# Seven block products of a feed-forward layer: which one comes second, and where the residual rows wait meanwhile

## The chip, the cores and the metric

The kernel runs on one core of one Trainium2 chip. The metric is the device time of one execution in microseconds (us). The engines are TensorE (PE, matrix products; its weight loads are PEld), VectorE (DVE), ScalarE (ACT), GpSimd (POOL) and SyncE (SP), which issues most transfers. Sixteen DMA engines move the data of all queues between device memory and the on-chip memory.

## The reference, cut to what matters

The program is two transformer-like blocks, one after the other, on 512 tokens of width 1024: a mixer block with a mixture of 16 experts, then a block with recurrent branches, a feed-forward layer and a gated embedding. All of it is in float32. The change touches the feed-forward layer of the second block and what stands around it:

```python
D_MODEL, SEQ, PLE_DIM = 1024, 512, 256
D_FF = -(-(8 * D_MODEL) // (3 * 256)) * 256            # 2816
...
    mixed = jax.nn.sigmoid(gate_a) * y_a + jax.nn.sigmoid(gate_b) * y_b
    x = x + mixed @ w_out

    h = _rmsnorm(x, g_ffn)
    x = x + (jax.nn.silu(h @ w1) * (h @ w3)) @ w2      # up products, then the down product

    gate = jax.nn.sigmoid(_rmsnorm(x, g_ple) @ w_ple_gate)
    x = x + gate * (p_i @ w_ple)
    return x                                           # then _rmsnorm(x, g_final)
```

## The kernel before, in words

**Order of the work.** The program is written out by hand for each engine; engines meet only at semaphores. In the profile the experts' matmuls run from 285 to 1190 us, the up products (`h @ w1`, `h @ w3`) from 1638 to 1877 us, the down product (`@ w2`) from there to 1993 us, and the gate product, the final norm and the stores to the end.

**Three passes.** A float32 product is made of three products of rounded numbers. For each operand ACT writes a rounded copy ("high part", `weight_rounded`, `down_rounded`), DVE the difference ("rest", `weight_rest`, `down_rest`), and PE adds high x rest, rest x high and high x high. So a piece of weights that lands must pass ACT, then DVE, before PE can use it.

**The down product** (512 x 2816 times 2816 x 1024) is split 2 x 2 x 2: into 256 tokens, 1408 inner, 512 output columns. Instead of eight block products it makes seven, after Strassen and Winograd, named `p1`, `ue`, `p2`, `wb`, `vg`, `zf`, `hh`. Each is 66 matmuls of 128 x 512 (11 inner tiles, 2 token tiles, 3 passes), in three chunks d = 0, 1, 2 of 24, 24 and 18 matmuls. PE counts a finished chunk in `down_chunk`, so p1's are 1 to 3, the second product's are 4 to 6, and so on. Before its first matmul a chunk waits for its rests (`wlo_made` for weights, `alo_made` for activations).

**Weights.** Blocks of `w2` lie in device memory as three pieces each: two of 128 x 2048 numbers (1024 KB, 1.05 MB) and one of 128 x 1536 (768 KB, 0.79 MB). `p1`, `p2` and `wb` use blocks 0, 2 and 3 as they are ("plain"). Their pieces go through a ring of four slots (`slot(c)`, c % 4): SP issues piece c on its hardware queue when piece c - 4 has been used. `ue`, `vg`, `zf` and `hh` use sums of blocks ("grown"). Those are made by the DMA itself: SP loads one block's piece into `grown[d]` or `joined[d]`, and POOL then issues an accumulating transfer on its own, software, queue (`add_weights`, L717 to L719), which adds a second block to what lies there. `ue` is block 0 + block 1; `vg` adds block 3 to that; `zf` is block 1 + block 3, in `joined`; `hh` adds block 2 to `vg`'s. That makes 12 accumulating transfers, in this order on POOL's queue: three for `ue`, three for `vg`, three for `zf`, three for `hh`, each waiting until its piece has landed and the previous use's rest has been made.

**Where things lie.** The residual rows `x_res` (512 x 1024, 2.1 MB) lie at `LOW`. During the up products they are written aside to device memory (`x_aside`, L2263 to L2265), and `grown[0]` and `grown[1]` are loaded onto their place (L2266 to L2271) and block 1 is added, in the middle of the up products. When the last up product is done, SP loads the rows back to another place (`x_late`, L2272 to L2274), that of the up products' inputs. `grown[2]` lies on a place that p1's rounded activations of chunks 0 and 1 use, so its load waits for `down_chunk` 2 (L2250 to L2253), and its sum for that load.

**ACT and DVE in the down stage.** Both go through the products in order, chunk by chunk: ACT rounds the activations (`round_part`, L2024), then the weights (`round_down`, L2031); DVE makes the two rests (L1626, L1633). From the third product on, ACT's rounded activations overwrite those of a product two before, so it waits until that one is done. DVE also adds finished products to the rows (`down_sums`, L1636 on).

The names that the steps touch: the tuple `DOWN` (L66) sets the order of the products on every engine; SP's loop over pieces is L2244 to L2289.

## Time and profile before

| | us |
|---|---|
| median of 3 runs | 2046.92 (2045.06 to 2048.33) |
| the profiled execution | 2047.97 |
| its span in the profile | 2046.2 |
| PE busy (matmuls) | 1940.0 (95%) |
| DVE / ACT / POOL busy | 787.7 / 543.2 / 126.2 |

The page gives for each engine the busy time in the span and, in 40 slices, how it is spread, with PE's granted clock and the share of the 16 DMA engines that is busy. The profiled execution took 1.77 us more than its span, and 1.05 us more than the median of the three runs. PE is the engine with most to do, but a busy share over the whole span hides single waits; the views used below are the busy time by windows, the timeline of single instructions, the queues' shares, and the issues of transfers.

### The profile page before, as it was taken

To read this page: it belongs to the slowest core of one execution; us is meant where nothing else is said; L and a number is where in the kernel's file an instruction comes from. 1 tells how busy PE (TensorE), PEld (TensorE's weight loads), DVE (VectorE), ACT (ScalarE), POOL (GpSimd) and SP (SyncE) were. 2 spreads that over 40 slices of the span, in tenths; PEclk is the share of its full clock that TensorE was granted. 3 is DMA by queue.
4 is the path that set the end of the run, shared out by engine and by line. 5 is a ranking of instruction groups with operands and counts; after the bars stand their busy time and mean duration, and the time that the engine had idled before them with its cause. 6 is when DMAs were issued, how large, how long until landed. Compare 5 with 4: busy or idle time off the path is not lost.

```text
span 2046.2 us, 22768 instructions
## 1 busy us (share of the span) xinstructions
PE 1940.0 (95%) x9356; PEld 1202.1 (59%) x9356; DVE 787.7 (38%) x1147; ACT 543.2 (27%) x840; POOL 126.2 (6%) x139
## 2 busy tenths in 40 slices
PE   8999999999899897998989799999999999999998
PEld 6868843333233332333333268878888888888786
DVE  6747331101101010100101057595587544446584
ACT  5246320101010000101000046323444332223465
POOL 3432000000000000000000000042000000000100
PEclk9998999999999999999999899999999999999999
DMA  9420789999999999999999943212124223533971
GB/s 274 144 73 17 295 325 429 432 430 426 433 431 429 431 430 429 432 431 428 432 431 429 425 158 144 69 56 65 61 83 144 83 100 127 164 123 113 268 196 66
DMA packets 45513, 534.90 MB, mean 261 GB/s; under 512 B 5488, under 2 KB 5616, under 8 KB 15104
## 3 DMA queue, kind: packets, MB, share of 16 engines
q1 hardware_dynamic: 41216, 514.42, 61.3%
q0 software_dynamic: 4224, 19.46, 4.5%
q8 instruction: 52, 0.85, 0.2%
q14 instruction: 21, 0.17, 0.0%
HBM read 524.39 MB, written 8.39 MB: 260 GB/s over the span
## 4 chain that ended last, share of the span: by engine, by line
PE 64%; DMA 23%; issue 7%; DVE 4%; ACT 1%; SPq 0%; POOL 0%; ACTq 0%; DVEq 0%; POOLq 0%
DMA arena<-in_w_gu_dram 21%; PE bank L2793 14%; PE bank L2818 5%; PE bank L745 3%; PE bank L747 3%; PE bank L746 3%; PE bank L2755 2%; PE bank L1106 2%; PE bank L1107 2%; PE bank L1108 2%; PE bank L2419 2%; PE bank L2421 2%; PE bank L2425 2%; DMA arena<-in_wpack_dram 2%; PE bank L1151 1%
## 5 line engine op out<-in xcount | busy, mean ns | idle before, releaser
L2793 PE MATMUL bank<-arena 128*64 128x512 f32 x2048 | 477.4, 621 | 71.3 <-DMA arena<-in_w_gu_dram 68.4
L2793 PEld LDWEIGHTS bank<-arena 128*64 128x64 f32 x2048 | 161.8, 143 | 362.1 <-issue 349.8
L3290 DVE TENSOR_TENSOR arena<-arena,bank 128x256 f32<-128x256 f32 x64 | 27.0, 421 | 640.3 <-ACT arena L3531 640.3
L2818 PE MATMUL bank<-arena 128*64 128x512 f32 x1024 | 232.5, 595 | 0.6 <-ACT arena L3535 0.6
L3531 ACT ACTIVATE arena<-bank 128x256 f32<-128x256 f32 x64 | 24.6, 384 | 537.7 <-PE bank L2793 537.7
L2818 PEld LDWEIGHTS bank<-arena 128*64 128x64 f32 x1024 | 73.4, 137 | 139.4 <-issue 139.4
L1106 PE MATMUL bank<-input_rounded,weight_rest 128*128 128x512 f32 x352 | 137.1, 390 | 0.0
L1108 PE MATMUL bank<-input_rounded,weight_rounded 128*128 128x512 f32 x352 | 137.0, 389 | 0.0
L1107 PE MATMUL bank<-input_rest,weight_rounded 128*128 128x512 f32 x352 | 136.9, 389 | 0.0
L745 PE MATMUL bank<-input_rounded,weight_rest 128*128 128x512 f32 x312 | 125.8, 403 | 0.0
L747 PE MATMUL bank<-input_rounded,unit_rounded 128*128 128x512 f32 x312 | 122.0, 391 | 0.0
L746 PE MATMUL bank<-mix_rest,unit_rounded 128*128 128x512 f32 x312 | 121.9, 391 | 0.0
L3535 ACT ACTIVATE arena<-bank 128x256 f32<-128x256 f32 x64 | 24.6, 384 | 214.9 <-PE bank L2804 214.9
L1108 PEld LDWEIGHTS bank<-input_rounded,weight_rounded 128*128 128x128 f32 x352 | 66.1, 188 | 13.9
L1106 PEld LDWEIGHTS bank<-input_rounded,weight_rest 128*128 128x128 f32 x352 | 66.1, 188 | 13.6
L1107 PEld LDWEIGHTS bank<-input_rest,weight_rounded 128*128 128x128 f32 x352 | 66.1, 188 | 13.6
L1776 ACT ACTIVATE unit_rounded<-arena 128x1024 fp32r<-128x1024 f32 x45 | 47.3, 1059 | 77.7 <-PE bank L747 62.1
L1570 DVE TENSOR_TENSOR weight_rest<-arena,weight_rounded 128x2048 fp32r<-128x2048 f32 x22 | 50.3, 2292 | 45.7 <-ACT weight_rounded L1996 45.7
L745 PEld LDWEIGHTS bank<-input_rounded,weight_rest 128*128 128x128 f32 x312 | 58.9, 189 | 13.1 <-issue 1.3
L747 PEld LDWEIGHTS bank<-input_rounded,unit_rounded 128*128 128x128 f32 x312 | 58.7, 188 | 12.9
L1200 DVE TENSOR_TENSOR weight_rest<-arena,unit_rounded 128x1024 fp32r<-128x1024 f32 x43 | 53.3, 1244 | 33.2 <-ACT unit_rounded L1776 33.1
L746 PEld LDWEIGHTS bank<-mix_rest,unit_rounded 128*128 128x128 f32 x312 | 59.0, 189 | 11.2
(584 smaller groups left out, 2940.7 us busy)
## 6 DMA issues: line engine op xcount, KB each, us to landing
arena<-in_w_gu_dram SPq DMA_DIRECT2D x47, 4096.0 KB, 28.9
arena<-in_w_d_dram SPq DMA_DIRECT2D x62, 2048.0 KB, 26.6
arena<-in_wpack_dram SPq DMA_DIRECT2D x81, 1024.0 KB, 5.3
arena<-in_w_gu_dram SPq DMA_DIRECT2D x32, 2048.0 KB, 17.8
arena<-in_wpack_dram POOLq DMA_DIRECT2D x8, 1024.0 KB, 12.2
arena<-in_w_d_dram SPq DMA_DIRECT2D x4, 1024.0 KB, 10.2
arena<-in_wpack_dram SPq DMA_DIRECT2D x5, 768.0 KB, 10.7
arena<-in_w_gu_dram SPq DMA_DIRECT2D x3, 1024.0 KB, 8.6
```

The source lines that it names most:

```text
L745: mm(b, wl[:, k, :], hhi[k], start=k == 0, stop=False)
L746: mm(b, wh[:, k, :], chlo[k], start=False, stop=False)
L747: last = mm(b, wh[:, k, :], hhi[k], start=False, stop=k == KD - 1)
L1106: mm(b, wl[:, k, m], hhi[k], start=k == 0, stop=False)
L1107: mm(b, wh[:, k, m], hlo[k], start=False, stop=False)
L1108: last = mm(b, wh[:, k, m], hhi[k], start=False, stop=k == KD - 1)
L1200: tt(out=unit_lo(j), in0=unit_raw(j), in1=unit_hi(j), op=ALU.subtract).then_inc(S("ulo_made"), 1)
L1570: tt(out=wlo[(c + which) % R], in0=w, in1=whi[(c + which) % R], op=ALU.subtract)\
L1776: fn(unit_hi(j), unit_raw(j), ACT.Copy).then_inc(S("uhi_made"), 1)
L2419: mm(b, wh[:, k, m], hhi[k], start=k == 0, stop=False)
L2793: last = mm(ab[64 * x:64 * x + 64, :], xsT[:, k, 64 * x:64 * x + 64], w[x][k], start=k == 0, stop=k == KD - 1)
L2818: last = mm(bank[4 + n][64 * x:64 * x + 64, :], hidT[c % 2][:, P * t + 64 * x:P * t + 64 * x + 64], w[:, x, t, 512 * n:512 * n + 512], sta ...
```

## The change

`p2`, a product with plain weights, comes second, and `ue`, with grown weights, third. The residual rows are no longer written aside: `x_res` stays at `LOW` for the whole layer and every later use reads it there (`x_late` is gone, and with it one transfer of 2.1 MB each way). `grown[0]` and `grown[1]` therefore lie where the up products' inputs were, and are loaded only after the last up product, directly after p1's third piece; POOL's first three accumulating transfers follow their landings. The rounded activations of `p2`, `ue`, `wb` and `vg` change places with one another. `joined[0]`'s load also waits for the first sum in `grown[0]`, and `joined[2]`'s moves from before `wb`'s second piece to behind `joined[1]`'s. Counts of `down_added` follow the order of the sums. The diff, without the further renamings of `x_late` to `x_res`:

```diff
--- before.py
+++ after.py
@@ -63,7 +63,7 @@
 BLK = HT * TOK
 
 
-DOWN = ("p1", "ue", "p2", "wb", "vg", "zf", "hh")
+DOWN = ("p1", "p2", "ue", "wb", "vg", "zf", "hh")
 DOWN_GROWN = ("ue", "vg", "zf", "hh")
 DOWN_WEIGHT = {"p1": 0, "p2": 2, "wb": 3}
 DOWN_KS = (range(0, 4), range(4, 8), range(8, HT))
@@ -184,7 +184,7 @@
     "pool_landing2": (("fnet_in", 80), ("added_in2", 64)),
     "landing1": (("xT_in1", 16), ("half_in1", 16), ("last_in1", 16), ("grown_in1", 32)),
     "landing3": (("first_in0", 16), ("place_in", 16), ("x_back", 16)),
-    "landing4": (("first_in1", 16), ("x_parked", 16), ("x_late_in", 16), ("ple_back", 16)),
+    "landing4": (("first_in1", 16), ("ple_back", 16)),
     "landing5": (("first_in2", 16), ("gfin_in", 16)),
     "landing6": (("xT_in3", 16), ("wple_in", 16), ("grown_in2", 32)),
     "landing2": (("xT_in2", 16), ("extra_in", 48)),
@@ -210,7 +210,6 @@
         bank += [two_banks[:, 0:512], two_banks[:, 512:1024]]
         named = {}
         ple_kept = nc.dram_tensor("ple_kept", (P, NT * D), F32, kind="Internal").ap()
-        x_aside = nc.dram_tensor("x_aside", (NT, P, D), F32, kind="Internal").ap()
         x_kept = nc.dram_tensor("x_kept", (NT, P, D), F32, kind="Internal").ap()
 
         def S(name):
@@ -524,7 +523,7 @@
         part_of = {"p1": "a11", "ue": "u", "p2": "a12", "wb": "w", "vg": "v", "zf": "z", "hh": "a22"}
         part_lo = {m: [rounded(f"down_rest_{m}_{d}", part_at[name] + TOK * ks[0], TOK * len(ks)) for d, ks in enumerate(DOWN_KS)]
                    for m, name in part_of.items()}
-        hi_at = {"ue": T0 + 1280, "p2": part_at["a11"], "wb": part_at["u"], "vg": part_at["a12"], "zf": part_at["w"],
+        hi_at = {"p2": T0 + 1280, "ue": part_at["a11"], "wb": part_at["a12"], "vg": part_at["u"], "zf": part_at["w"],
                  "hh": part_at["v"]}
         part_hi = {m: [rounded(f"down_rounded_{m}_{d}", at + TOK * ks[0], TOK * len(ks)) for d, ks in enumerate(DOWN_KS)]
                    for m, at in hi_at.items()}
@@ -532,9 +531,8 @@
                      (6, 7, rounded("down_rounded_p1_6", B + 19712, TOK)), (7, 8, rounded("down_rounded_p1_7", T0 + 256, TOK)),
                      (8, 11, rounded("down_rounded_p1_8", T0 + 512, 3 * TOK))]
         first_his_upto = (1, 4, 5)
-        grown = [view(LOW, WCH), view(LOW + WCH, WCH), view(LOW + 9088, 3 * 512)]
+        grown = [view(LOW + 4096, WCH), view(LOW + 4096 + WCH, WCH), view(LOW + 9088, 3 * 512)]
         joined = [view(T0 + 512, WCH), view(B, WCH), view(T0 + 2560, 3 * 512)]
-        x_late = view(LOW + 4096, NT, D)
         pieces = [view(B + 19712 + 512 * i, 512) for i in range(2)]
         down_bank = {"p1": (4, 5), "ue": (6, 7), "p2": (2, 3), "wb": (4, 5), "vg": (0, 1), "zf": (2, 3), "hh": (0, 1)}
 
...
@@ -1125,7 +1123,7 @@
             def turn_tokens(half, ks):
                 for k in ks:
                     for i in range(2):
-                        last = turn(turned_place(half, k)[:, P * i:P * i + P], x_late[:, 2 * half + i, P * k:P * k + P], ident)
+                        last = turn(turned_place(half, k)[:, P * i:P * i + P], x_res[:, 2 * half + i, P * k:P * k + P], ident)
                     last.then_inc(S("norm_turned"), 1)
 
             for m, name in enumerate(DOWN):
@@ -1138,7 +1136,7 @@
                             pe.wait_ge(S("p1_copied"), nth("p1_copied", 2))
                             pe.wait_ge(S("down_added"), nth("down_added", 2))
                         elif name == "zf":
-                            pe.wait_ge(S("down_added"), nth("down_added", 8))
+                            pe.wait_ge(S("down_added"), nth("down_added", 4))
                         elif name == "hh":
                             pe.wait_ge(S("down_added"), nth("down_added", 12))
                     pe.wait_ge(S("alo_made"), rests_upto(m, d))
...
@@ -1643,7 +1641,6 @@
                 b = [bank[j][:, :] for j in down_bank[name]]
                 dve.wait_ge(S("down_chunk"), 3 * m + 3)
                 if name == "p1":
-                    dve.wait_ge(S("x_late_in"), nth("x_late_in", 16))
                     for i in range(2):
                         dve.wait_ge(S("p1_copied"), nth("p1_copied", i + 1))
                         add_down(out_part(i, 0), out_part(i, 0), b[i], ALU.add)
@@ -1657,7 +1654,7 @@
                     for i in range(2):
                         add_down(out_part(i, 0), out_part(i, 0), b[i], ALU.add)
                 elif name == "wb":
-                    dve.wait_ge(S("down_added"), nth("down_added", 6))
+                    dve.wait_ge(S("down_added"), nth("down_added", 8))
                     for i in range(2):
                         add_down(out_part(i, 1), out_part(i, 1), b[i], ALU.subtract)
                 elif name == "vg":
...
@@ -2260,24 +2257,18 @@
                         .then_inc(S(f"chunk_in{c % R}"), 16)
                 else:
                     sp.dma_start(slot(c), wpack[from_dram(c)]).then_inc(S(f"chunk_in{c % R}"), 16)
-                if c == C_UP + 9:
-                    sp.wait_ge(S("out2_added"), nth("out2_added", 8))
-                    sp.dma_start(x_aside.rearrange("i p d -> p i d"), x_res).then_inc(S("x_parked"), 16)
-                if c == C_UP + 13:
-                    sp.wait_ge(S("norm_turned"), 2 * KD)
-                    sp.wait_ge(S("norm_sq"), NT * (N4 + 1))
-                    sp.wait_ge(S("x_parked"), nth("x_parked", 16))
+                if c == C_DOWN + 2:
+                    sp.wait_ge(S("up_filled"), 2 * NFT)
                     for d in range(2):
                         sp.dma_start(grown[d], wpack[C_DOWN + d]).then_inc(S(f"grown_in{d}"), 16)
-                if c == C_DOWN + 2:
-                    sp.wait_ge(S("up_filled"), 2 * NFT)
-                    sp.dma_start(x_late, x_aside.rearrange("i p d -> p i d")).then_inc(S("x_late_in"), 16)
                 if c == C_DOWN + 9:
-                    for d in (0, 2):
-                        sp.dma_start(joined[d], wpack[C_DOWN + 3 + d][:, 0:512 * len(DOWN_KS[d])]).then_inc(S(f"grown_in{d}"), 16)
+                    sp.wait_ge(S("added_in0"), nth("added_in0", 16))
+                    sp.dma_start(joined[0], wpack[C_DOWN + 3]).then_inc(S("grown_in0"), 16)
                 if c == C_DOWN + 11:
                     sp.wait_ge(S("down_chunk"), 9)
-                    sp.dma_start(joined[1], wpack[C_DOWN + 4]).then_inc(S("grown_in1"), 16)
+                    for d in (1, 2):
+                        sp.wait_ge(S(f"added_in{d}"), nth(f"added_in{d}", 16))
+                        sp.dma_start(joined[d], wpack[C_DOWN + 3 + d][:, 0:512 * len(DOWN_KS[d])]).then_inc(S(f"grown_in{d}"), 16)
                 if c == C_OUT2 + 1:
                     sp.wait_ge(S("oT_filled"), 8)
                     sp.wait_ge(S("x_kept"), 16 * NT)
```

SP's issues from p1's third piece (128x1536, the first row) to the load of `joined[1]` (the last row); in brackets the semaphores waited for. Before:

```order
L2259 DMA arena<-in_wpack_dram 128x1536 [waits up_filled]
L2274 DMA arena<-x_aside 128x4x1024 [waits up_filled]
L2253 DMA arena<-in_wpack_dram 128x1536 [waits down_chunk]
L2259 DMA arena<-in_wpack_dram 128x2048 [waits down_chunk] x2
L2259 DMA arena<-in_wpack_dram 128x1536 [waits down_chunk]
L2259 DMA arena<-in_wpack_dram 128x2048 [waits down_chunk]
L2277 DMA arena<-in_wpack_dram 128x2048
L2277 DMA arena<-in_wpack_dram 128x1536
L2259 DMA arena<-in_wpack_dram 128x2048 [waits down_chunk]
L2259 DMA arena<-in_wpack_dram 128x1536 [waits down_chunk]
L2280 DMA arena<-in_wpack_dram 128x2048 [waits down_chunk]
```

Here L2274 is the load of the residual rows and L2253 that of `grown[2]`. After:

```order
L2256 DMA arena<-in_wpack_dram 128x1536 [waits up_filled]
L2263 DMA arena<-in_wpack_dram 128x2048 [waits up_filled]
L2263 DMA arena<-in_wpack_dram 128x2048
L2256 DMA arena<-in_wpack_dram 128x2048 [waits up_filled]
L2256 DMA arena<-in_wpack_dram 128x2048 [waits down_chunk]
L2256 DMA arena<-in_wpack_dram 128x1536 [waits down_chunk]
L2250 DMA arena<-in_wpack_dram 128x1536 [waits down_chunk]
L2256 DMA arena<-in_wpack_dram 128x2048 [waits down_chunk]
L2266 DMA arena<-in_wpack_dram 128x2048 [waits pool_landing0]
L2256 DMA arena<-in_wpack_dram 128x2048 [waits down_chunk]
L2256 DMA arena<-in_wpack_dram 128x1536 [waits down_chunk]
L2271 DMA arena<-in_wpack_dram 128x2048 [waits pool_landing1,down_chunk]
```

L2263 is now the loads of `grown[0]` and `grown[1]`. They stand ahead of the next row, the first piece of the second product, which waits for no chunk of the down stage; its second and third piece wait for `down_chunk` 1 and 2. `grown[2]` (L2250) stands behind them, and one `joined` load fewer (L2266, L2271) stands ahead of `wb`'s second piece.

On ACT, from p1's third weight piece (`weight_rounded_120`, 117, 118, ... are the four slots of the high parts) to the copy of p1's result. Before:

```order
L2024 ACTIVATE down_rounded_ue_142<-arena 128x1024 [waits up_filled,dve_parts]
L2031 ACTIVATE weight_rounded_118<-arena 128x2048 [waits pool_landing0,up_filled]
L2024 ACTIVATE down_rounded_ue_143<-arena 128x1024 [waits up_filled,dve_parts]
L2031 ACTIVATE weight_rounded_119<-arena 128x2048 [waits pool_landing1,down_chunk]
L2024 ACTIVATE down_rounded_ue_144<-arena 128x768 [waits up_filled,dve_parts]
L2031 ACTIVATE weight_rounded_120<-arena 128x1536 [waits pool_landing2,down_chunk]
L2060 ACTIVATE arena<-bank 128x512 [waits act_made,down_chunk]
L2060 ACTIVATE arena<-bank 128x512
L2024 ACTIVATE down_rounded_p_0_145<-arena 128x1024 [waits down_chunk,dve_parts]
L2031 ACTIVATE weight_rounded_117<-arena 128x2048 [waits chunk_in0]
```

After:

```order
L2021 ACTIVATE down_rounded_p_0_142<-arena 128x1024 [waits up_filled,dve_parts]
L2028 ACTIVATE weight_rounded_118<-arena 128x2048 [waits chunk_in1]
L2021 ACTIVATE down_rounded_p_1_143<-arena 128x1024 [waits up_filled,dve_parts]
L2028 ACTIVATE weight_rounded_119<-arena 128x2048 [waits chunk_in2]
L2021 ACTIVATE down_rounded_p_2_144<-arena 128x768 [waits up_filled,dve_parts]
L2028 ACTIVATE weight_rounded_120<-arena 128x1536 [waits chunk_in3]
L2057 ACTIVATE arena<-bank 128x512 [waits act_made,down_chunk]
L2057 ACTIVATE arena<-bank 128x512
L2021 ACTIVATE down_rounded_ue_145<-arena 128x1024 [waits down_chunk,dve_parts]
L2028 ACTIVATE weight_rounded_117<-arena 128x2048 [waits pool_landing0,down_chunk]
```

The weights of the second product's chunks wait for ring pieces (`chunk_in`) in place of POOL's sums (`pool_landing`); the copies of p1's result and then `ue` stand behind them.

## Rows read from the trace of the kernel before

**Rows 1.** Windows: busy us (xinstructions) by engine, PEclk, DMA share, GB/s.

```profile
1750.00:1876.00 126.00, 126.00 (x558) 104.33 (x557) 63.01 (x79) 30.07 (x26) 1.75 (x2) 1.00 0.37 129
1892.90:1914.40 21.50, 17.48 (x67) 13.96 (x66) 9.22 (x8) 8.68 (x8) 3.45 (x4) 0.84 0.97 247
1908.00:1913.00 5.00, 5.00 (x12) 3.94 (x13) 5.00 (x5) 5.00 (x4) 0.84 (x1) 0.52 1.05 276
```

**Rows 2.** Timeline of PE, down stage: start us, us, instruction, [idle, releaser].

```profile
1892.90 0.39 PE L1151 MATMUL bank<-weight_rounded,down_rest_ue 128*128 128x512 f32 x1
...
1903.55 0.39 PE L1153 MATMUL bank<-weight_rounded,down_rounded_ue 128*128 128x512 f32 x1
...
1907.96 0.76 PE L1151 MATMUL bank<-weight_rounded,down_rest_ue 128*128 128x512 f32 x1 [4.02 <-DVE weight_rest L1633]
...
1913.06 0.40 PE L1151 MATMUL bank<-weight_rounded,down_rest_ue 128*128 128x512 f32 x1
...
1914.44 0.40 PE L1151 MATMUL bank<-weight_rounded,down_rest_p 128*128 128x512 f32 x1
...
1935.21 0.47 PE L1151 MATMUL bank<-weight_rounded,down_rest_wb 128*128 128x512 f32 x1 [0.20 <-DVE weight_rest L1633]
```

**Rows 3.** Timeline of ACT, down stage.

```profile
1882.94 1.49 ACT L2031 ACTIVATE weight_rounded<-arena 128x1536 fp32r<-128x1536 f32 x1 [2.21 <-DMA arena<-in_wpack_dram]
...
1904.54 1.48 ACT L2031 ACTIVATE weight_rounded<-arena 128x1536 fp32r<-128x1536 f32 x1 [13.87 <-DMA arena<-in_wpack_dram]
...
1930.82 1.92 ACT L2031 ACTIVATE weight_rounded<-arena 128x2048 fp32r<-128x2048 f32 x1 [3.96 <-DMA arena<-in_wpack_dram]
```

**Rows 4.** Timeline of DVE, down stage.

```profile
1932.77 2.29 DVE L1633 TENSOR_TENSOR weight_rest<-arena,weight_rounded 128x2048 fp32r<-128x2048 f32 x1 [3.40 <-ACT weight_rounded L2031]
```

**Rows 5.** Timeline of SP, the hardware queue's issues; a row of several spans all.

```profile
1747.21 0.80 SPq L2262 DMA_DIRECT2D arena<-in_wpack_dram  x2
1748.13 1.05 SPq L2271 DMA_DIRECT2D arena<-in_wpack_dram  x2
...
1877.77 0.33 SPq L2259 DMA_DIRECT2D arena<-in_wpack_dram  x1
...
1878.14 0.43 SPq L2274 DMA_DIRECT2D arena<-x_aside  x1
...
1920.09 5.77 SPq L2259 DMA_DIRECT2D arena<-in_wpack_dram  x2
```

**Rows 6.** Timeline of POOL, issues of the accumulating transfers.

```profile
1757.23 0.90 POOL L718 DMA_DIRECT2D arena<-in_wpack_dram  x1 [335.89 <-DMA arena<-in_wpack_dram]
1759.69 0.85 POOL L718 DMA_DIRECT2D arena<-in_wpack_dram  x1 [1.57 <-DMA arena<-in_wpack_dram]
1893.63 2.60 POOL L718 DMA_DIRECT2D arena<-in_wpack_dram  x3 [133.09 <-DMA arena<-in_wpack_dram]
...
1926.96 0.86 POOL L718 DMA_DIRECT2D arena<-in_wpack_dram  x1 [17.77 <-DMA arena<-in_wpack_dram]
```

**Rows 7.** DMA queues from 1751 to 1757 us: packets, MB, share of 16 engines.

```profile
q1 hardware_dynamic: 354, 2.51, 99.2%
```

**Rows 8.** DMA queues from 1761 to 1769 us.

```profile
q0 software_dynamic: 219, 1.66, 102.7%
```

**Rows 9.** DMA queues from 1903 to 1915 us.

```profile
q0 software_dynamic: 230, 1.73, 69.3%
q1 hardware_dynamic: 233, 1.56, 32.5%
```

**Rows 10.** DMA queues from 1921 to 1929 us.

```profile
q1 hardware_dynamic: 482, 3.28, 97.4%
q0 software_dynamic: 23, 0.05, 3.1%
```

**Rows 11.** DMA issues from 1757 to 1758 us: size each, us to landing.

```profile
arena<-in_wpack_dram POOLq DMA_DIRECT2D x1, 1024.0 KB, 7.8
```

**Rows 12.** DMA issues from 1903 to 1904.5 us.

```profile
arena<-in_wpack_dram SPq DMA_DIRECT2D x1, 768.0 KB, 13.3
```

More of the change, by code:

```diff
@@ L1635, in out_part @@
             def out_part(i, n):
-                return x_late[:, i, 512 * n:512 * n + 512]
+                return x_res[:, i, 512 * n:512 * n + 512]
             def add_down(out_, in0, in1, op):
@@ L1730, in second_dve @@
                 own.wait()
-                xs = x_late[:, i, 512 * n:512 * n + 512]
+                xs = x_res[:, i, 512 * n:512 * n + 512]
                 tt(out=xs, in0=xs, in1=g, op=ALU.add).then_inc(S("pg_added"), 1)
@@ L1734, in second_dve @@
                     dve.wait_ge(S("pg_added"), nth("pg_added", 7))
-                    own(tt(out=hn[:, NT - 1, 0:512], in0=x_late[:, NT - 1, 0:512], in1=grow[:, 0:512], op=ALU.mult))
-                    own(tt(out=hn[:, i, :], in0=x_late[:, i, :], in1=grow, op=ALU.mult))
+                    own(tt(out=hn[:, NT - 1, 0:512], in0=x_res[:, NT - 1, 0:512], in1=grow[:, 0:512], op=ALU.mult))
+                    own(tt(out=hn[:, i, :], in0=x_res[:, i, :], in1=grow, op=ALU.mult))
                     norm_var(dve, NO, i)
@@ L1758, in second_dve @@
                     norm_rstd(dve, own, NO, i)
-                    stt(out=hn[:, i, :], in0=x_late[:, i, :], scalar=nstat[NO][:, i:i + 1], in1=grow, op0=ALU.mult,
+                    stt(out=hn[:, i, :], in0=x_res[:, i, :], scalar=nstat[NO][:, i:i + 1], in1=grow, op0=ALU.mult,
                         op1=ALU.mult).then_inc(S("out_made"), 1)
@@ L2040, in down_square @@
                 act.wait_ge(S("norm_sq"), NT * N5 + i)
-                act.activation(junk, x_late[:, i, :], ACT.Square, accum_out=nstat[N5][:, i:i + 1]).then_inc(S("norm_sq"), 1)
+                act.activation(junk, x_res[:, i, :], ACT.Square, accum_out=nstat[N5][:, i:i + 1]).then_inc(S("norm_sq"), 1)
             for f in range(NFT):
@@ L2086, in second_act @@
                     act.wait_ge(S("pg_added"), nth("pg_added", 6))
-                    own(fn(junk[:, 0:512], x_late[:, NT - 1, 0:512], ACT.Square, accum_out=v))
+                    own(fn(junk[:, 0:512], x_res[:, NT - 1, 0:512], ACT.Square, accum_out=v))
                     own.wait()
@@ L2100, in second_act @@
                     act.wait_ge(S("norm_sq"), NT * NO + i)
-                    fn(junk[:, 512:D], x_late[:, i, 512:D], ACT.Square, accum_out=stat[:, 342:343]).then_inc(S("norm_sq"), 1)
+                    fn(junk[:, 512:D], x_res[:, i, 512:D], ACT.Square, accum_out=stat[:, 342:343]).then_inc(S("norm_sq"), 1)
                     act.wait_ge(S("norm_var"), NT * NO + NT)
@@ L2109, in second_act @@
                     v = nstat[NO][:, i:i + 1]
-                    fn(junk, x_late[:, i, :], ACT.Square, accum_out=v).then_inc(S("norm_sq"), 1)
+                    fn(junk, x_res[:, i, :], ACT.Square, accum_out=v).then_inc(S("norm_sq"), 1)
                     if i < NT - 2:
```

## The prediction

> **What bounds the kernel now.** I read the page first: PE is busy 95% of the span, so only PE's waits and its pace count. Then the busy time by windows. In the up products PE is busy 126.0 of 126.0 us, with the 16 DMA engines at 0.37 [rows 1]: the transfer that parks the residual rows and the first sums run there beside PE and cost nothing, so taking them out gives nothing there. In the window of `ue` PE is busy 17.5 of 21.5 us, while the DMA share is 0.97. Then the timeline of PE: 48 matmuls start between 1892.90 and 1903.55, one per 0.227 us, so a product of 66 should take 15.0 us. `ue` takes 1914.44 - 1892.90 = 21.5 us, 6.6 us too much [rows 2]. Of it 4.0 us is a wait for DVE's rest of the third piece, and DVE waited for ACT, ACT 13.9 us for the DMA [rows 3]. After the wait the granted clock is 0.52 over 5 us [rows 1], the lower level of 1.2 GHz: the 12 matmuls from 1907.96 to 1913.06 take 5.1 us for 2.7, another 2.4 us. The only other wait in the stage is 0.2 us at `wb`'s second chunk, whose piece was issued at 1920.09 and landed at 1930.82, 10.7 us later [rows 2, 3, 5]. So PE bounds the stage, and its waits are set by transfers.
>
> **What the change removes.** The wait at `ue`'s third chunk and its clock loss: 6.6 us. `ue` now starts a product later, while its third piece is still loaded at `down_chunk` 2, 15 us more in which to land and be summed. With 15 us against a wait of 4.0 I take this term in full.
>
> The load of the parked rows (2.1 MB) goes from the start of the stage, but `grown[0]` and `grown[1]` (2.1 MB) take its place in the queue, and their two sums come into the stage. That is the price, and I work it out at three places.
>
> **Prices of a transfer.** The hardware queue alone moves 2.51 MB in 6 us at 99% share, 0.418 MB/us, so a piece of 1.05 MB takes 2.5 us [rows 7]. Sums alone move 1.66 MB in 8 us at a full share, 0.208 MB/us [rows 8]: 5.0 us a piece, twice as much of the same engines. Together they got 0.130 (hardware) and 0.144 MB/us (sums) over 12 us [rows 9]: a plain piece then takes 8.1 us, 5.6 us more than alone. From landing to PE a piece of 1.05 MB takes 4.4 us through ACT and DVE (1930.82 to 1935.21), one of 0.79 MB 3.4 us (1904.54 to 1907.96) [rows 2 to 4].
>
> **Place A, p2's first piece.** The order on SP is now p1's third piece, `grown[0]`, `grown[1]`, then this piece. The same pattern of four loads stands in the up products: issued from 1747.21 on, the third landed at 1757.23 and the fourth at 1759.69 (POOL's issues follow the landings) [rows 5, 6]. From 1877.77, with the first load 0.79 MB (0.6 us less), the fourth lands 11.9 us later, at 1889.6. PE can start `p2` at 1894.0 and wants it at 1892.9: wait 1.1 us. This holds if the first sum, issued at about 1884.7 when `grown[0]` lands, does not slow it. In two places a sum came late into a busy hardware queue: issued at 1926.96, the sums moved only 0.05 MB between 1921 and 1929 against 3.28 MB [rows 6, 10]. So I take 1.1 us; bounds 1.1 and 6.7 (5.6 us more).
>
> **Place B, p2's second piece.** Undisturbed it lands 2.5 us later, 1892.1, and is ready before its time (1894.0 + 5.4 = 1899.4): 0. But now two sums of 1.05 MB, 10 us of engine time, are in flight. At the shared rate it is 5.6 us later: 1897.7, PE at 1902.1, a wait of 2.7 us. I take 2.7, the nearest row being the shared one [rows 9]; bounds 0 and 4. The third piece lands 0.79 / 0.130 = 6.1 us after that, 1903.8, ready at 1907.2, wanted at 1907.5: just covered. `ue`'s first weights stand behind it on ACT; between 1903.8 and `ue`'s turn at 1911.6 ACT has 1.5 + 1.9 us and DVE 2.3 us of weights to do [rows 3, 4] and three small steps: I cost it at nothing, at most 1 us.
>
> **Place C, wb's second piece.** It is issued when the product before `wb` has done its first chunk, three chunks (15.0 us) before its use, so it may take 15.0 - 4.4 = 10.6 us to land. Before it took 10.7 (the 0.2 us wait), with the sums silent for 8 of these us [rows 10]. Now POOL cannot issue `vg`'s three sums before `ue`'s rests are made, 15 us later than before, so their 2.9 MB (14 us of engine time alone, 20 us at the shared rate) fall on this load; against this, one load of 0.79 MB fewer stands ahead. The slowest load that shared with sums took 13.3 us [rows 12]: wait 2.7, of which 0.2 was there, so 2.5 us. Bounds: 0, and 6.4, if the three loads (3.15 MB) run at 0.130 MB/us until the sums end after 20 us and then alone, landing 17 us after the issue.
>
> The whole ledger says the same. From 1879 to the landing of `wb`'s third piece the engines had 11.3 MB of loads and 3.7 MB of sums, 27.0 + 17.7 = 44.7 us of work; now it is 10.5 and 5.8 MB, 25.1 + 27.8 = 52.9 us. Without any wait that piece would be wanted at 1892.9 + 15.0 + 15.0 + 10.9 - 3.4 = 1930.4, 51.4 us after 1879. Before, there were 6.7 us to spare, now none. `wb`'s third piece I cost at nothing beyond this, since a wait at the second gives it that time. The later sums (`zf`, `hh`) have the queue to themselves in both kernels; they move with PE, and I take 0.
>
> **Clock.** A wait of 4.0 us cost 2.4 us of lower clock; 0.2 us cost none [rows 2]. For waits of 1.1, 2.7 and 2.7 us nothing shows it; bounds 0 and 4.8, I take one fall, 2.4 us.
>
> **The sum.** 1.1 + 2.7 + 2.5 + 2.4 = 8.7 us added, 6.6 us removed: +2.1 us. On the profiled execution's own 2047.97 that gives 2050.1; it stands 1.05 above the median of the runs, so against 2046.92 I predict 2049.0.
>
> **Rival 1: the loads keep ahead of the sums.** If sums only get what a busy hardware queue leaves, as from 1921 to 1929 [rows 10], B, C and the clock cost nothing: 1.1 - 6.6 = -5.5 us, 2041.4. Against it: from 1903 to 1915 the sums took 69% of the engines [rows 9]. The Trainium skill ("DMA: Bandwidth & Descriptors", on the anatomy of one DMA on the GpSimd path) fits 2.0 us plus bytes over 436 GB/s for such a transfer, 4.4 us for 1.05 MB. By that the sums' work would halve, the ledger would close, and this rival would be likely; the trace has 7.8 us for one accumulating transfer with little beside it [rows 11], and the measurement decides.
>
> **Rival 2, slower: the first sum shares from its start.** It begins 1.5 us after its issue (7.8 us to landing less 5.0 us of data leaves 2.8 for both ends [rows 8, 11]), at 1886.2, just when p2's first piece gets its turn. That piece then lands at 1895.2, PE starts `p2` at 1899.6: A is 6.7. The second piece lands at 1902.4, when the two sums (14.6 us) have ended, ready 1906.8 for 1905.0: B 1.8. With C 2.5 and two clock falls 4.8: 15.8 - 6.6 = +9.2, 2056.1. It decides from where p2's first piece lands after 1890. For it: the equal split in [rows 9]; against it the late start in [rows 10]. The Trainium skill ("DMA: Bandwidth & Descriptors", "Queues, rings and completion order") has each engine take turns between its queues packet by packet; by this rule the result is this rival's. The trace agrees with it from 1903 to 1915 and not from 1921 to 1929.
>
> **Rival 3: the change moves the wait but not away from ue.** POOL sums in order, so `ue`'s third sum stands behind two others; issued at some 1907 and 7.8 us long, it lands at 1915, ready 1918.4 for 1922.5. If it missed by the 4 us that it has, the old wait would be back and the prices with it: about +6, 2053.
>
> **How the numbers follow.** Three runs of this kernel spread over 0.16%, so 0.2% (4.1 us) is about what a measurement can tell. Forecast 0.42, its own range from -2 (B and the clock nothing) to +6 (C at its bound): 0.34 of it lies within 0.2%, 0.08 above. Rival 1 0.25: 0.21 faster, 0.04 the same. Rival 2 0.27 and rival 3 0.06, slower. That makes faster 0.21, same 0.38, slower 0.41. The range reaches to rivals 1 and 2, 2041 to 2056.5.
>
> **What would show it.** Right: no PE wait before `ue`'s third chunk; a short wait before p2's first chunk; waits before p2's second and `wb`'s second chunk of 2 to 3 us with a window of clock 0.5 behind one; the up products unchanged at 126 of 126 us; the DMA share near 1 from 1880 to 1937. Wrong: p2's first piece landing after 1890 (rival 2), or its second by 1895 and `wb`'s second within 10.7 us of its issue (rival 1). If PE waits in `zf` or `hh`, the cover that I counted there is gone.

## The result and the profile after

| | us |
|---|---|
| before, median of 11 runs | 2047.45 (2045.06 to 2049.66) |
| after, median of 11 runs | 2053.67 (2049.1 to 2055.01) |
| ratio after / before | 1.0025, 95% interval 1.0017 to 1.0033 |
| the profiled executions | 2047.97 and 2053.49 |
| their spans | 2046.2 and 2051.7 |

The change makes the kernel slower by 0.25%, 5.1 us on the 2046.92 shown before it (the medians alone differ by 6.2). 2049.0 was predicted: the sign of the sum was right, its size too small.

"Stage" below is the time from SP's issue of p1's third piece to the end of `zf`'s third chunk. It grew from 98.97 us to 103.42 us, by 4.46 us. The other 1.07 us of the 5.5 us between the two profiled executions lie ahead of the stage, which begins at 1878.84 for 1877.77 [rows 5]. In the profiled executions of four kernels below that keep the rows parked, and so do the same work as before up to there, it begins between 1877.42 and 1880.04; so the 1.07 us are within the scatter of single executions and no effect of the change.

Windows of after (columns as in [rows 1]): a stretch of the up products, p2's waits, the end of the wait in `wb`, the matmuls right behind it, and all stretches up to there.

```profile
1750.00:1876.00 126.00, 126.00 (x558) 104.36 (x557) 63.23 (x80) 30.06 (x26) 0.00 (x0) 1.00 0.26 99
1893.90:1913.60 19.70, 15.50 (x68) 12.23 (x66) 12.84 (x10) 11.56 (x11) 0.85 (x1) 1.00 0.88 221
1928.80:1949.00 20.20, 15.51 (x62) 12.44 (x61) 10.15 (x9) 11.15 (x9) 0.85 (x2) 0.92 0.99 280
1939.00:1943.00 4.00, 3.83 (x10) 3.14 (x11) 1.89 (x3) 2.51 (x3) 0.00 (x0) 0.57 1.05 298
1880.00:1937.00 57.00, 50.20 (x217) 40.05 (x215) 32.62 (x28) 25.94 (x22) 6.00 (x7) 1.00 0.95 276
```

The up products run exactly as before, 126.00 of 126.00 us [rows 1]; the share of the DMA engines there fell from 0.37 to 0.26. In the last row, from 1880 to 1937, that share is 0.95.

PE's timeline in after, all rows of the stage up to `vg` with a wait for a DVE rest:

```profile
1896.57 0.47 PE L1149 MATMUL bank<-weight_rounded,down_rest_p 128*128 128x512 f32 x1 [2.44 <-DVE weight_rest L1631]
...
1904.03 0.47 PE L1149 MATMUL bank<-weight_rounded,down_rest_p 128*128 128x512 f32 x1 [1.75 <-DVE weight_rest L1631]
...
1939.17 0.77 PE L1149 MATMUL bank<-weight_rounded,down_rest_wb 128*128 128x512 f32 x1 [4.69 <-DVE weight_rest L1631]
```

These are the places A, B and C of the prediction, and no others: `ue`, `zf` and `hh` wait for nothing. Against [rows 2], where `ue` waited 4.02 us, the wait at `ue` is gone, A and B are new, and the wait at C has grown from 0.20 us. Behind C the matmuls run at the lower level of the clock (0.57 in the window): eight of them take 3.5 us for 1.9, so 1.6 us are lost. Behind A and B the clock stays at its full level here.

ACT in after, at the landings behind A, B (its first two rows) and C (the last row):

```profile
1892.18 1.92 ACT L2028 ACTIVATE weight_rounded<-arena 128x2048 fp32r<-128x2048 f32 x1 [5.79 <-DMA arena<-in_wpack_dram]
...
1899.64 1.92 ACT L2028 ACTIVATE weight_rounded<-arena 128x2048 fp32r<-128x2048 f32 x1 [4.60 <-DMA arena<-in_wpack_dram]
...
1920.04 1.92 ACT L2028 ACTIVATE weight_rounded<-arena 128x2048 fp32r<-128x2048 f32 x1 [3.01 <-DMA arena<-in_wpack_dram]
...
1934.79 1.91 ACT L2028 ACTIVATE weight_rounded<-arena 128x2048 fp32r<-128x2048 f32 x1 [11.88 <-DMA arena<-in_wpack_dram]
```

SP in after; L2263 issues `grown[0]` and `grown[1]`, L2266 `joined[0]`, and the row at 1919.55 is `wb`'s second and third piece:

```profile
1878.84 0.33 SPq L2256 DMA_DIRECT2D arena<-in_wpack_dram  x1
1879.21 0.91 SPq L2263 DMA_DIRECT2D arena<-in_wpack_dram  x2
1880.16 10.25 SPq L2256 DMA_DIRECT2D arena<-in_wpack_dram  x3
...
1913.85 0.33 SPq L2256 DMA_DIRECT2D arena<-in_wpack_dram  x1
1914.22 0.43 SPq L2266 DMA_DIRECT2D arena<-in_wpack_dram  x1
1919.55 5.77 SPq L2256 DMA_DIRECT2D arena<-in_wpack_dram  x2
```

POOL in after; the first two rows are `ue`'s first two sums, the last three `vg`'s:

```profile
1886.73 0.90 POOL L716 DMA_DIRECT2D arena<-in_wpack_dram  x1 [464.32 <-DMA arena<-in_wpack_dram]
1889.22 0.85 POOL L716 DMA_DIRECT2D arena<-in_wpack_dram  x1 [1.59 <-DMA arena<-in_wpack_dram]
...
1914.18 0.84 POOL L716 DMA_DIRECT2D arena<-in_wpack_dram  x1 [5.37 <-DVE weight_rest L1631]
1917.52 0.85 POOL L716 DMA_DIRECT2D arena<-in_wpack_dram  x1 [2.50 <-DVE weight_rest L1631]
1920.06 0.85 POOL L716 DMA_DIRECT2D arena<-in_wpack_dram  x1 [1.68 <-DVE weight_rest L1631]
```

The three sums of `vg`, each released by a rest of `ue`, stand around the issue of `wb`'s second piece at 1919.55; before, POOL was silent for the first 7 us after that issue [rows 6]. The queues of after from 1916 to 1934:

```profile
q0 software_dynamic: 295, 2.15, 58.0%
q1 hardware_dynamic: 432, 3.10, 44.4%
```

Both together fill the engines (102%), with the sums taking more than half of the share for less than half of the bytes. This window begins before the sums move. From 1920 to 1934 alone, the sums have 278 packets and 69% of the engines, the hardware queue 273 packets and 34%. The piece issued at 1919.55 lands at 1934.79, 15.2 us later, for 10.7 before [rows 3, 5]. That is place C.

### The profile page after: what moved, and what is told of

Its sections match the earlier page's. It is cut to its first block, busy times and chain, and to the rows that moved or that the text cites. A ratio compares the mean times of both kernels' runs of the same rounds, so it can differ in the third digit from the quotient of the medians.

```text
span 2051.7 us, 22766 instructions
## 1 busy us (share of the span) xinstructions
PE 1939.9 (95%) x9356; PEld 1203.6 (59%) x9356; DVE 788.9 (38%) x1147; ACT 543.5 (26%) x840; POOL 126.0 (6%) x139
## 4 chain that ended last, share of the span: by engine, by line
PE 71%; DMA 23%; DVE 4%; ACT 1%; issue 1%; SPq 0%; ACTq 0%; DVEq 0%
DMA arena<-in_w_gu_dram 21%; PE bank L2784 14%; PE bank L2809 5%; PE bank L1104 4%; PE bank L1105 4%; PE bank L1106 4%; PE bank L743 3%; PE bank L745 3%; PE bank L744 3%; PE bank L2746 2%; PE bank L2410 2%; PE bank L2412 2%; PE bank L2416 2%; DMA arena<-in_wpack_dram 1%; PE bank L1149 1%; PE bank L1150 1%
## 6 DMA issues: line engine op xcount, KB each, us to landing
arena<-in_w_d_dram SPq DMA_DIRECT2D x62, 2048.0 KB, 26.6
arena<-in_w_gu_dram SPq DMA_DIRECT2D x32, 2048.0 KB, 16.7
```

## The experiments

Each kernel ran on the same chip as the kernel before, in three groups; before had medians of 2048.25, 2048.0 and 2048.17 us there. Kernels of different groups are best compared by their ratios to before (0.1% is 2 us). "Waits" are PE's in the stage. Stage and waits come from one profiled execution of each kernel, which can lie some us from the median: 3.9 us above it for after with the sums held, 3.3 and 3.2 us below it for rows stay alone and for `vg`'s sums small.

| kernel | median us | ratio to before, 95% | stage us | waits us |
|---|---|---|---|---|
| before | 2047.45 | | 98.97 | ue 4.02, wb 0.20 |
| after | 2053.67 | 1.0025 (1.0017 to 1.0033) | 103.42 | p2 2.44, 1.75; wb 4.69 |
| order alone | 2050.38 | 1.0011 (1.0002 to 1.0020) | 100.96 | p2 1.84; wb 4.00 |
| rows stay alone | 2053.67 | 1.0028 (1.0019 to 1.0037) | 103.92 | ue 5.03, 0.64; p2 0.20, 0.56; wb 1.90 |
| after, plain piece first | 2053.31 | 1.0029 (1.0018 to 1.0039) | 103.78 | p2 0.45; ue 0.17; wb 8.36 |
| after, grown loads later | 2052.69 | 1.0024 (1.0015 to 1.0033) | 102.61 | ue 3.21; wb 5.57 |
| after, `joined[0]` later | 2048.63 | 1.0006 (0.9997 to 1.0014) | 99.50 | p2 2.37, 0.18; wb 0.65; vg 1.36 |
| after, ue's sums small | 2048.39 | 1.0001 (0.9992 to 1.0010) | 99.47 | p2 1.67; wb 2.26, 1.22 |
| after, vg's sums small | 2047.36 | 0.9992 (0.9983 to 1.0001) | 96.75 | p2 2.32, 1.76 |
| order alone, vg's sums held | 2045.67 | 0.9992 (0.9983 to 1.0001) | 96.97 | p2 1.80; vg 1.08 |
| after, vg's sums held | 2052.81 | 1.0020 (1.0011 to 1.0028) | 106.54 | p2 2.25, 1.81; wb 6.52 |
| order, held, plain first, joined later | 2044.66 | 0.9982 (0.9973 to 0.9990) | 95.95 | wb 2.13 |
| the same, joined last | 2041.41 | 0.9965 (0.9953 to 0.9978) | 93.06 | vg 0.91 |
| the same, rows stay | 2045.97 | 0.9992 (0.9983 to 1.0000) | 96.81 | p2 0.26, 0.19, 0.22; wb 1.71; vg 1.16 |

**1. The change in two halves.** Order alone: before with the new order, and the rows still parked.

```diff
-DOWN = ("p1", "ue", "p2", "wb", "vg", "zf", "hh")
+DOWN = ("p1", "p2", "ue", "wb", "vg", "zf", "hh")
```

> The kernel before with one part of the change: p2 second and ue third (with the places of the rounded activations and of the joined loads that this asks for). The residual rows are still parked in device memory and grown[0] and grown[1] are still loaded and summed during the up products. Theory T (the order pays for itself; the price of the change is the two grown loads and their two sums, moved into the stage): no wait at p2 (0 instead of 2.4 and 1.8 us in the changed kernel) and none at ue, wb's second chunk waits 0 to 2 us; 5 to 7 us faster than before, about 2041.5. Theory U (the order itself costs, since vg's sums now fall on wb's pieces): wb's second chunk still waits 4 to 5 us and the clock falls, so about the time before, 2046 to 2048.

Rows stay alone: after with the old tuple, so the rows stay, and grown loads and their sums fall into the stage.

> The other half of the change alone: the residual rows stay on chip, grown[0] and grown[1] are loaded and summed from the end of the up products, but ue stays second. Theory T: ue's first sum lands some 17 us after the end of the up products, so PE waits about 6 us before ue's first chunk and about 4 us before its third, with the clock falling behind each; later waits as before: 6 to 10 us slower than before, about 2055. If the parked rows' transfers cost anything, less by that. With the order alone at +2.1 us, a sum of the two halves would be +8 to +12 us; the changed kernel has +5 to +6, so the order should save part of what the late sums cost.

Order alone did not gain: it is 0.11% slower. It frees `ue` of its wait, but `wb`'s first piece, issued at 1911.84, lands at 1926.38, 14.5 us later, beside the three sums that `ue`'s rests have just released. PE, then POOL, of order alone:

```profile
1930.77 0.76 PE L1151 MATMUL bank<-weight_rounded,down_rest_wb 128*128 128x512 f32 x1 [4.00 <-DVE weight_rest L1633]
```

```profile
1907.37 0.84 POOL L718 DMA_DIRECT2D arena<-in_wpack_dram  x1 [7.85 <-DVE weight_rest L1633]
1910.70 0.85 POOL L718 DMA_DIRECT2D arena<-in_wpack_dram  x1 [2.50 <-DVE weight_rest L1633]
1913.24 0.84 POOL L718 DMA_DIRECT2D arena<-in_wpack_dram  x1 [1.68 <-DVE weight_rest L1633]
```

So the wait of 4.0 us was moved to `wb`, clock loss included, by the order and without the grown loads. Neither theory had the 1.84 us at p2's first chunk. There is no sum beside that piece; it stands behind the load of the rows, 2.1 MB, and lands 12.7 us after the start of the stage. In after it stands behind the grown loads, also 2.1 MB, and lands after 13.3 us.

Rows stay alone costs 0.28%; `ue` waits 5.03 us at its first chunk, about as expected, but only 0.64 us at its third for some 4. With both, the cost is no larger than with the second alone: the order takes `ue` out of the way of its late sums, and gives that back in `wb`.

**2. Places A and B.** In the first kernel p2's first piece goes ahead of the grown loads, in the second these go behind all three of p2's pieces.

```diff
-                if c == C_DOWN + 2:
+                if c == C_DOWN + 3:      # grown loads later: C_DOWN + 5
                     sp.wait_ge(S("up_filled"), 2 * NFT)
                     for d in range(2):
                         sp.dma_start(grown[d], wpack[C_DOWN + d])...
```

> The changed kernel with p2's first piece issued ahead of the loads of grown[0] and grown[1]. Theory T (the queue's order and its sharing with the sums decide): the wait before p2's first chunk (2.4 us) is gone, but p2's second piece still stands behind the two grown loads, so its wait grows from 1.8 to about 4.2 us and the time stays within 1 us of the changed kernel (or 1 to 2 us slower if the clock falls). If only the first piece mattered, 2.4 us faster than the changed kernel.

> The changed kernel with the loads of grown[0] and grown[1] behind all three pieces of p2 (they are then issued at down_chunk 2, some 11 us later). Theory T: both waits of p2 are gone (4.2 us); ue's first sum lands some 4 us before it is wanted, so ue does not wait; wb's second chunk waits as in the changed kernel, 4 to 6 us with the clock falling: 3 to 4.5 us faster than the changed kernel, about 2049.7. Rival (the sums are late now): ue waits 2 to 5 us and nothing is gained.

With the plain piece first, 4.19 us of waits at p2 become 0.45, and with the later loads none. So A and B come from what stands ahead of p2's pieces and runs beside them. For A that is mostly the 2.1 MB ahead: with the order alone the wait is 1.84 us, and with `ue`'s sums small (in 3) it is 1.67. B is the sums: with them small it is gone, with the grown loads in place. Neither of the two kernels here helped the time. In the first the wait came back in `wb`, whole; in the second it came back at `ue` (3.21 us) and in `wb` (5.57). PE of plain piece first:

```profile
1938.94 0.77 PE L1149 MATMUL bank<-weight_rounded,down_rest_wb 128*128 128x512 f32 x1 [8.36 <-DVE weight_rest L1631]
```

8.36 is 4.69 plus the 3.7 us gained earlier, and `wb`'s second chunk starts 60.5 us into the stage for 60.3. With PE earlier, the pieces have no less work of the engines ahead of them. This is what the prediction's ledger says (52.9 us of work for 51.4 us of time). The expectation of the first kernel had the time right and the place wrong (p2's second chunk); in the second kernel the rival came true.

**3. Place C.** Three kernels take something from beside `wb`'s second piece. First `joined[0]`'s load, moved from ahead of that piece to behind `wb`'s third:

```diff
-                if c == C_DOWN + 9:
-                    sp.wait_ge(S("added_in0"), nth("added_in0", 16))
-                    sp.dma_start(joined[0], wpack[C_DOWN + 3])...
                 if c == C_DOWN + 11:
+                    sp.wait_ge(S("added_in0"), nth("added_in0", 16))
+                    sp.dma_start(joined[0], wpack[C_DOWN + 3])...
```

> The changed kernel with the load of joined[0] moved from ahead of wb's second piece to behind wb's third. Theory T1 (wb's second piece is late because 3.15 MB stand in its queue while the sums take two thirds of the engines): it lands 5 to 8 us sooner than the 15.2 us after its issue, the wait of 4.7 us and the 1.5 us of lower clock are gone: about 6 us faster than the changed kernel, 2047.5. Rival T2 (the sums alone delay it): it still takes over 12 us and the wait is 2 us or more, 2 to 3 us faster.

Then the size of the sums, where `n` is the number of columns that a sum covers, 128 in place of 2048 or 1536. Such a kernel leaves out most of the block to be added, so its result is another; only its times are of use:

```diff
-                add_weights(grown[d], 1, d)
+                add_weights(grown[d], 1, d, n=128)      # ue's, or instead:
-                add_weights(grown[d], 3, d)
+                add_weights(grown[d], 3, d, n=128)      # vg's
```

> The changed kernel with ue's three sums (block 1) made on 128 of the 2048 columns only, so the second product's weights stay nearly plain and that part of the result is another; all loads, waits and issues stand as before. Theory T: the sums, not the grown loads, make p2's second piece late, so its wait (1.8 us) goes; the first piece is late mostly by the queue ahead of it, so 1 to 2.4 us of its wait stays; wb's second piece keeps its wait of 4 to 5 us: 1.5 to 3 us faster than the changed kernel. Rival (the loads ahead alone): nothing changes.

> The changed kernel with vg's three sums (block 3) made on 128 columns only, so vg, and hh with it, are computed with other weights. Theory V (vg's sums, which now run beside wb's plain loads, are the price of the new order): wb's second piece lands within 9 us of its issue, and its wait of 4.7 us with 1.5 us of lower clock goes: 6 us faster than the changed kernel. Rival J (the joined load ahead of it is the cause): it still takes over 12 us and 2 us or more of the wait stay.

All three are faster than after, by 0.19%, 0.24% and 0.33% of before, some 4 to 7 us. With `joined[0]` later the wait falls to 0.65 us: the piece, issued at 1918.32, lands 11.2 us after its issue.

```profile
1929.51 1.92 ACT L2028 ACTIVATE weight_rounded<-arena 128x2048 fp32r<-128x2048 f32 x1 [8.30 <-DMA arena<-in_wpack_dram]
```

That lies between the two theories (7 to 10 us, and over 12). B is nearly gone in this profile too (0.18 us), but by accident: the clock fell behind A, and PE came 1.6 us later to the second chunk. With `vg`'s sums small it lands by 5.1 us after its issue and `wb` doesn't wait, while A and B stand as they were and `joined[0]` is still ahead. So C needs `vg`'s sums; `joined[0]` alone does not make it, but beside the sums it adds most of the wait. ACT of after with `vg`'s sums small; the piece of the second row was issued at 1916.76:

```profile
1915.91 1.92 ACT L2029 ACTIVATE weight_rounded<-arena 128x2048 fp32r<-128x2048 f32 x1 [1.43 <-DMA arena<-in_wpack_dram]
1921.88 1.92 ACT L2029 ACTIVATE weight_rounded<-arena 128x2048 fp32r<-128x2048 f32 x1 [3.11 <-DMA arena<-in_wpack_dram]
```

With `ue`'s sums small I expected 1.5 to 3 us and got 5 (0.24%): less work early in the stage also reaches `wb`, whose waits are 3.5 us for 4.69. Each of the three brings the kernel back to about the time before; they were not run together, so their gains can't be taken to add.

**4. The sums held.** The rests of `ue` need not release `vg`'s sums at once, since `vg` comes two products later. POOL's second and third sum of `vg` now wait for chunks of PE:

```diff
                 pool.wait_ge(S("wlo_made"), NFT + 3 * DOWN.index("ue") + d + 1)
+                if d:
+                    pool.wait_ge(S("down_chunk"), 6 + d)
                 add_weights(grown[d], 3, d)
```

> The kernel with the order alone (p2 second, rows parked), in which POOL issues vg's second sum only at down_chunk 7 and the third at down_chunk 8 (there they came at about 2 us before and 1 us after down_chunk 6 and wb's first piece took 14.5 us to land). Theory V: wb's first piece lands within 10 us, its wait of 4.0 us and the 2.4 us of clock go, vg and hh still find their sums: 5 to 6 us faster than the order alone, 3 to 4 us faster than before. Rival (the engines are short in all, so the held sums are missed later): waits of about the same sum at vg, zf or hh, no gain over the order alone.

> The changed kernel in which POOL issues vg's second sum at down_chunk 7 and the third at down_chunk 8 at the earliest (they came at +3.7 and +6.2 us after down_chunk 6). Theory V: here the sums are later anyway, so the holding moves them by only 2 and 5 us; wb's second piece, with joined[0] ahead of it, gains 1 to 4 us of its wait of 4.7: 1 to 5 us faster than the changed kernel. Rival: nothing, since the three sums still overlap its load.

On the kernel with the order alone this gained 0.19% of before, 3.9 us (the medians, from two groups, differ by 4.7). Against before itself (0.9983 to 1.0001) it can't be told apart. Its POOL, then ACT at the landing of `wb`'s first piece:

```profile
1905.32 0.84 POOL L718 DMA_DIRECT2D arena<-in_wpack_dram  x1 [7.86 <-DVE weight_rest L1635]
1917.40 0.85 POOL L718 DMA_DIRECT2D arena<-in_wpack_dram  x1 [11.24 <-PE bank L1155]
1922.84 1.72 POOL L718 DMA_DIRECT2D arena<-in_wpack_dram  x2 [4.58 <-PE bank L1155]
```

```profile
1916.19 1.92 ACT L2033 ACTIVATE weight_rounded<-arena 128x2048 fp32r<-128x2048 f32 x1 [3.64 <-DMA arena<-in_wpack_dram]
```

`wb`'s first piece, issued at 1911.42, landed at 1916.19, 4.8 us later for 14.5, with POOL issuing nothing from 1906.2 to 1917.4. On after, the same edit gave nothing that can be told apart (0.20% for 0.25%, the intervals overlap), and the wait at `wb` is 6.52 us where I expected it to shrink. That profile is of the slowest of its 12 executions, 2056.73 us, with one more fall of the clock, at p2, so it can't be said that the wait grew in all of them. `joined[0]` and the late sums of `ue` may fill the time that holding frees; this was not tested.

**5. A kernel that beats both.** The order alone, the sums held, p2's first piece ahead of the rows' load (`C_DOWN + 3`, as in 2), and `joined[0]` behind `wb`'s second piece; then the same with `joined[0]` behind `wb`'s third (as in 3); then that with the rows staying on chip.

> As the kernel with the order alone and the sums held, and besides p2's first piece is issued ahead of the load of the parked rows (wait 1.8 us there) and joined[0] behind wb's second piece. Theory V and the queue's order: no wait of over 0.5 us is left in the stage; it is 6 to 7 us shorter than before, time about 2041. Rival: the engines are short and a wait of 2 us or more appears at vg, zf or hh.

> The kernel with the order alone, vg's sums held, p2's first piece ahead of the parked rows, and now joined[0] behind wb's third piece (it stood between the second and the third, and the third waited 2.1 us). Theory: that wait goes and none over 1.4 us comes at vg or zf; 0.5 to 2 us faster than with joined[0] in between, stage 94 to 95.5 us where before had 99.0. Rival: the late joined[0] delays zf's and hh's sums and the wait comes back at vg, zf or hh.

> The changed kernel (rows stay) with the same three moves: p2's first piece ahead of the grown loads, vg's second and third sum held, joined[0] behind wb's third piece. Theory: with two more sums (10 us of the engines) in the stage the waits at p2's second piece (4 us) and one at wb or vg of 1 to 3 us stay, about 2046 to 2048, 2 to 4 us slower than the same moves with parked rows. Rival (the moves are enough, the two sums fit): as fast as with parked rows, about 2043.

The first missed its expectation by the place of one load: 2.13 us of wait at `wb`'s third piece, and 1.6 us of lower clock behind it. The second has this window for its whole stage, a PE wait of 0.91 us in it, and the lowest time:

```profile
1879.64:1972.70 93.06, 92.07 (x413) 75.89 (x412) 74.77 (x66) 56.95 (x53) 8.48 (x10) 1.00 0.85 235
```

Its 2041.41 us (2039.91 to 2043.89 over 5 runs) is 0.35% below before. The third is this kernel with the other half of the change, and 4.6 us slower, in spite of a transfer of 2.1 MB fewer each way: two loads and two sums of 1.05 MB stand in the stage in place of one load of 2.1 MB.

## Why the prediction was right or wrong

- **What is removed: right.** The wait at `ue` and its clock loss are gone, 6.6 us; taking the parking out of the up products gave nothing there. The order alone shows how little this is worth by itself: as much comes back in `wb`.
- **Place A: too small.** 1.1 us predicted, 2.44 measured, within the bounds. Counted from the start of the stage, p2's first piece landed after 13.3 us for a predicted 11.9. Of this, 0.8 us is there without any sum (12.7 us with the order alone), so the pattern of four loads in the up products was too fast a model; 0.6 us came with the grown loads and the first sum.
- **Place B: too large.** 2.7 predicted, 1.75 measured. From the start of the stage, p2's first chunk began 1.5 us later than predicted, which took as much of B's wait away. A and B together are 3.8 predicted and 4.2 measured; that the two errors nearly cancel is luck.
- **Place C: the term that failed in size.** The cause was as predicted. The step was "the slowest load that shared with sums took 13.3 us": it took 15.2, and the wait was 4.69 for 2.7. I took the row of a smaller piece (0.79 MB [rows 12]) at another place as it stood, where the piece here had 1.05 MB, three sums beside it, and ahead of it `joined[0]` and the last of `wb`'s first piece. The measured term, 4.5 us net of before's 0.2, lies between the value taken (2.5) and the bound worked out from these loads (6.4), about in the middle.
- **Clock: right in kind.** One fall, behind C as its wait came out, 1.6 us for 2.4. That it was only one is partly luck: behind a wait of 2.37 us at the same place as A the clock did fall with `joined[0]` later, and it didn't behind the 2.44 us here.
- **The sum.** 2.44 + 1.75 + 4.69 + 1.6 = 10.5 us of waits and clock, less before's 4.02 + 0.20 + 2.4 = 6.6, is +3.9 us; the stage grew 4.46. The remaining 0.6 us are not explained. The forecast's own range of -2 to +6 holds the result, but of its chances the 0.34 on "within 0.2%" lay on the wrong side of the line: the result, 0.25%, is a little above it. Of the 0.41 on "slower", 0.33 belonged to rivals 2 and 3, which both fell.
- **Rival 1** (loads keep ahead) fell: from 1916 to 1934 the sums had 58% of the engines, and `wb`'s second piece took 15.2 us. **Rival 3** fell: `ue` did not wait.
- **Rival 2** (the first sum shares from its start) fell by the size of A, 2.44 us and not 6.7, but half of its condition came true: p2's first piece did land after 1890. The queues of after from 1890 to 1898 show why this wasn't as dear:

```profile
q0 software_dynamic: 121, 0.99, 60.3%
q1 hardware_dynamic: 183, 1.23, 41.5%
```

The sum issued at 1886.73 moved its first packet at 1891.1, 4.4 us later, when that piece had almost landed. The rival had it begin 1.5 us after its issue, at 1888.2. The Trainium skill ("DMA: Bandwidth & Descriptors", "Queues, rings and completion order") has each engine take turns between its queues packet by packet. The trace agrees once the sum moves: from 1891.5 to 1898 the two queues have 114 and 120 packets. The late start does not follow from it, and no run shows its cause.
- **The ledger: right, and stronger than the terms built beside it.** It said that there was no time to spare before `wb`'s third piece. The experiments that removed A and B got all of it back as waits in `ue` and `wb`, and those that moved 1.05 MB of load behind `wb` or took most of 2.9 MB of sums away gained 4 to 7 us, early or late in the stage.

## What to carry to other kernels

When a product is moved in an order, look not only at what it waits for but at what its end releases: here the rests of `ue` released `vg`'s sums into the very time in which `wb`'s plain pieces load. Where the transfer engines are the scarce thing, a wait removed early comes back at the next late piece; what helps is less work for them, or work in the order of its deadlines. A sum made by an accumulating transfer cost twice a load's time on these engines (0.208 against 0.418 MB/us [rows 7, 8]), so here hiding two of them in a stage with idle engines was worth more than a transfer of 2.1 MB each way: the last two kernels of 5 differ by 4.6 us.

## What the runs showed of the hardware that was not expected

- An accumulating transfer issued into a busy hardware queue mostly starts to move data late: its first packet came 4.4 us after its issue in after (1886.73) and 3.9 us in before (1926.96), but only 1.6 us at 1757.23 in before, when the last load of the hardware queue was moving, and 1.5 to 1.6 us beside an idle queue (1907.96 in after). Once it moves, the two queues have equal counts of packets, and the sums take 69% of the engines beside 31 to 34% (after, 1891.5 to 1898 and 1920 to 1934).
- A plain piece of 1.05 MB, `wb`'s second, landed 11.2 us (`joined[0]` later), 15.2 us (after) and 19.2 us (plain piece first) after its issue beside sums; with `vg`'s sums small it took 5.1 us, and the first piece with the sums held 4.8 us.
- The length of a wait of PE did not decide alone whether the clock fell. Behind waits of 2.32, 2.44 and 3.21 us it stayed at the full level. Behind 1.80 us (order alone, sums held) and 2.37 us (after, `joined[0]` later) it fell to the lower level (granted clock 0.50) 0.4 to 1.5 us after PE had gone on, for about eight matmuls, 1.6 us lost. Behind those of 4.00, 4.69 and 8.36 us the first matmul is already slow, 0.76 or 0.77 us for 0.47. PE of after, `joined[0]` later; at the full level these start 0.23 us apart:

```profile
1895.36 0.47 PE L1149 MATMUL bank<-weight_rounded,down_rest_p 128*128 128x512 f32 x1 [2.37 <-DVE weight_rest L1631]
1895.67 0.53 PE L1150 MATMUL bank<-weight_rest,down_rounded_p 128*128 128x512 f32 x1
1896.00 0.63 PE L1151 MATMUL bank<-weight_rounded,down_rounded_p 128*128 128x512 f32 x1
1896.43 0.63 PE L1149 MATMUL bank<-weight_rounded,down_rest_p 128*128 128x512 f32 x1
```
